# Memory projections in two rounded parts, the gate's products between two weight slots, and the band attention ahead of the sparse one

## The reference, cut to what matters

```python
k = (mem @ w_k).reshape(B, M, X_HEADS, X_HEAD_DIM)   # cross_attention, for both layers: 1024 -> 512
v = (mem @ w_v).reshape(B, M, X_HEADS, X_HEAD_DIM)
...
gate = jnp.einsum('gpq,bnqgc->bnpgc', sgu_w, vg) + sgu_b.T[None, None, :, :, None]   # ab_mixer
b_out = neighbourhood_attention(q_l, k_l, v_l, k_c, v_c, rel_bias)                   # reads v_l, v_c
...
def even_mixer(x, w_in, ckv_gain, w_uk, w_uv, sinks, w_out, rel_table):
    q_a, c_kv, q_i, k_i, w_i, q_b, k_b, v_b = split_cols(x @ w_in, EVEN_WIDTHS)
    o_a = dsa_attention(q_a, c_kv, q_i, k_i, w_i, ckv_gain, w_uk, w_uv, rel_table[:, :A_HEADS])
    o_b = banded_attention(q_b, k_b, v_b, rel_table[:, A_HEADS:A_HEADS + B_HEADS], B_WINDOW, sinks)
    return jnp.concatenate([o_a, o_b], axis=-1) @ w_out
```

## Time and profile before

| | |
|---|---|
| Median of three runs | 2578.78 us (2578.42 to 2579.43) |
| The profiled execution | 2579.02 us |
| Its span, first to last instruction | 2577.2 us |
| Mean granted TensorE clock | 0.993 of 2.4 GHz |
| PE busy | 2508.4 us, 97% of the span |
| DVE busy | 1984.1 us, 77% |
| ACT busy | 1164.9 us, 45% |
| Time outside the span | 2579.02 - 2577.2 = 1.8 us |

### The profile page before, as it was taken

How to read it: one execution, slowest core, us unless ns; L and a number is a source line. 1 busy time by engine, 2 the same in 40 slices (tenths; PEclk the granted TensorE clock), 3 DMA queues, 4 the chain that set the end, 5 groups by cost and what they waited for, 6 DMA issues and landing times.

```text
span 2577.2 us, 42769 instructions
## 1 busy us (share of the span) xinstructions
PE 2508.4 (97%) x16883; PEld 2143.3 (83%) x16883; DVE 1984.1 (77%) x2452; ACT 1164.9 (45%) x1477; POOL 87.5 (3%) x109
## 2 busy tenths in 40 slices
PE   9999999999999999889999899999999999999998
PEld 6786788888789999789998688888888888888886
DVE  0875877777776886858887747888889888988887
ACT  1427200000431003532013736777777777777776
POOL 0100100000000001000001100000000000000000
PEclk9999999999999999999999999999999999999999
DMA  8771454444315553224545124999899989999996
GB/s 346 275 268 61 156 180 166 166 170 163 115 50 220 185 186 135 80 101 156 185 179 197 34 99 167 374 366 376 331 376 362 374 335 372 366 351 357 363 374 252
DMA packets 90969, 603.85 MB, mean 234 GB/s; under 512 B 9792, under 2 KB 12864, under 8 KB 23616
## 3 DMA queue, kind: packets, MB, share of 16 engines
q1 hardware_dynamic: 77424, 544.24, 56.0%
q0 software_dynamic: 13392, 57.41, 6.2%
HBM read 598.47 MB, written 3.15 MB: 233 GB/s over the span
## 4 chain that ended last, share of the span: by engine, by line
PE 90%; DVE 5%; ACT 2%; issue 1%; DMA 1%; DVEq 0%; SPq 0%; ACTq 0%
PE bank L1143 12%; PE bank L1147 12%; PE bank L1146 12%; PE bank L2354 8%; PE bank L2358 8%; PE bank L2357 8%; PE bank L2385 4%; PE bank L2389 4%; PE bank L2388 4%; PE bank L516 2%; ACT arena L1423 1%; PE bank L1796 1%; PE bank L1399 1%; PE bank L1378 1%; PE bank L556 1%
## 5 line engine op out<-in xcount | busy, mean ns | idle before, releaser
L941 DVE TENSOR_TENSOR ring_part<-ring,arena_part 128x2048 fp32r<-128x2048 f32 (+1 forms) x478 | 1073.2, 2276 | 23.8 <-ACT arena_part L960 9.3
L2689 ACT ACTIVATE arena_part<-ring 128x2048 fp32r<-128x2048 f32 x339 | 647.2, 1920 | 196.8 <-DMA ring<-in_stream 196.6
L1143 PE MATMUL bank<-arena_part 128*128 128x256 f32 (+1 forms) x2024 | 644.9, 319 | 4.6 <-DVE ring_part L941 4.6
L1147 PE MATMUL bank<-arena_part,ring_part 128*128 128x256 f32 (+1 forms) x2024 | 643.2, 318 | 0.0
L1146 PE MATMUL bank<-h_part,arena_part 128*128 128x256 f32 (+1 forms) x1496 | 474.9, 317 | 0.0
L1143 PEld LDWEIGHTS bank<-arena_part 128*128 128x128 f32 x2024 | 385.9, 191 | 33.0 <-issue 6.8
L1147 PEld LDWEIGHTS bank<-arena_part,ring_part 128*128 128x128 f32 x2024 | 385.9, 191 | 25.4
L2354 PE MATMUL bank<-arena_part,h_part 128*128 128x512 f32 x896 | 354.5, 396 | 0.0
L2358 PE MATMUL bank<-arena_part,h_part 128*128 128x512 f32 x896 | 350.0, 391 | 0.0
L2357 PE MATMUL bank<-ring_part,h_part 128*128 128x512 f32 x896 | 349.2, 390 | 0.0
L1245 ACT ACTIVATE arena<-bank 128x256 f32<-128x256 f32 (+1 forms) x66 | 30.1, 455 | 636.8 <-PE bank L1147 635.9
(11 more groups left out here) (364 smaller groups left out, 3090.5 us busy)
## 6 DMA issues: line engine op xcount, KB each, us to landing
ring<-in_stream SPq DMA_DIRECT2D x515, 1024.0 KB, 4.9
arena<-in_ada_stream POOLq DMA_DIRECT2D x80, 512.0 KB, 4.5
consts<-in_small POOLq DMA_DIRECT2D x1, 2800.0 KB, 11.7
mem_store<-arena POOLq DMA_DIRECT2D x2, 1024.0 KB, 13.1
arena<-in_c_rows POOLq DMA_DIRECT2D x2, 1024.0 KB, 7.1
arena<-in_ab_bias POOLq DMA_DIRECT2D x1, 2048.0 KB, 10.1
arena<-in_t_bias POOLq DMA_DIRECT2D x1, 2048.0 KB, 8.7
arena<-in_mem_t SPq DMA_DIRECT2D x1, 1024.0 KB, 5.0
```

Source lines behind the costliest of these rows:

```text
L941: return nc.vector.tensor_tensor(low, value, high.bitcast(F32), ALU.subtract)
L1143: m = nc.tensor.matmul(out_ap, w_high, high, start=start, stop=False)
L1147: return nc.tensor.matmul(out_ap, w_low, high, start=False, stop=stop)
L2689: nc.scalar.activation(high, ring[:, where], ACT.Copy).then_inc(sem("moe_high"), 1)
```

## The change

What it does, piece by piece:

1. **Start.** The memory (`mem_in`) is parted into `mem_high` (ACT, eight pieces) and `mem_low` (DVE, eight pieces). Seven of the eight memory slots are parted too; K1a alone stays in f32. V1a and V1b are now loaded behind K1b and ahead of A0, and all four of these slots ahead of x and the context. The turned modulation rows stand between the two halves of the last value products.
2. **AB mixer.** The sixteen gate products stand between slots AB8 and AB9 of the value products, and DVE works on the gate ahead of copying the values out. The gate waits for its own weights (`sgu_landed`); the attention's first value step waits for the copied values.
3. **Even mixer.** `w_idx` is multiplied among the split products of the third and fourth column. The index scores follow at once on the column of c, ahead of its sum of squares. k_b and v_b are copied by ACT, not by DVE. The band's three steps stand first in the attention (`N_BAND`), and the latent values behind its last step, in two parts.

```diff
-START = ["K1a", "K1b", "A0", "A1", "V1a", "V1b", "A2", "A3", "A4", "K0a", "A5", "A6", "A7", "K0b", "V0a", "V0b"]
+START = ["K1a", "K1b", "V1a", "V1b", "A0", "A1", "A2", "K0a", "A3", "A4", "K0b", "A5", "A6", "A7", "V0a", "V0b"]
...
+                        if rounded:
+                            m = split_product(bk, w, PS[b][:, X2], mem_high[:, k, :], mem_low[:, k, :], k == 0, k == DC - 1,
+                                              highs=mem_slot_high)
+                            continue
...
-            mem_key_products(range(4))
+            mem_key_products(range(2), rounded=False)
+            pe.wait_ge(sem("mem_split"), DC)
+            mem_key_products(range(2, 4))
+            mem_value_products()
...
+            act.wait_ge(sem("mem_landed"), 16)
+            for c in range(DC):
+                nc.scalar.activation(mem_high[:, c, :], mem_in[:, c, :], ACT.Copy).then_inc(sem("mem_rounded"), 1)
+            for name in ("K1b", "V1a", "V1b"):
+                slot_high_act(bk, START.index(name), mem_slot_high, fresh=True)
             act.wait_ge(sem("x_landed"), 32)
             squares_act(bk, TT, lambda c: None)
+            slot_high_act(bk, START.index("K0a"), mem_slot_high, fresh=True)
             root_act(bk, TT, 0)
+            slot_high_act(bk, START.index("K0b"), mem_slot_high, fresh=True)
+            act.wait_ge(sem("mem_stored1"), 16)
+            for name in ("V0a", "V0b"):
+                slot_high_act(bk, START.index(name), mem_slot_high, fresh=True)
...
+            split_token_products(bk, w, ab_high, h_part, 4, ab_slot_high, between=gate_products)
+            for taken in queries_keys_taken:
                 pe.wait_ge(*taken)
...
+            attention_pe(bk, ab_steps(), values_ready)
...
-            attention_pe(bk, dsa_steps() + band_steps(), latent_values)
+            outs = attention_pe(bk, band_steps() + dsa_steps(), sparse_ready)
+            for j, taken in enumerate(outs):
+                pe.wait_ge(*bk.freed(taken))
+                b = bk.fill(score_bank(j))
+                pe.wait_ge(free(b), bk.emptied())
+                for h in range(4 * j, 4 * j + 4):
+                    at = SEQ * (h // 2 % 2)
+                    m = nc.tensor.matmul(PS[b][half(h % 2), at:at + SEQ], uv[:, h, :], o_lat[:, h, :], start=True, stop=True)
+                m.then_inc(full(b), 1)
...
+            for n in range(4):
+                load(n)
```

More of the change, by code:

```diff
@@ L297, in build @@
         mem_store = [nc.dram_tensor(f"mem_store{l}", (P, 2048), F32, kind="Internal").ap() for l in range(2)]
+        mem_high, mem_low = (part_area(at, 2048, "p (c t) -> p c t", c=DC) for at in (22368, 4096))
+        mem_slot_high = {START.index(name): part_area(at, SLOT) for name, at in (
+            ("K1b", 10240), ("V1a", 12288), ("V1b", 15360), ("K0a", 17408), ("K0b", 10240), ("V0a", 20320), ("V0b", 2048))}
         MEM_BANKS, MEM_GROUPS = (6, 7), 6
@@ L1179, in split_token_products @@
             for k in range(DC):
+                if between and k == DC // 2:
+                    between()
                 r, j = w.t // TILES, k % per
@@ L1788, in mem_key_products, with mem_value_products @@
                     m.then_inc(full(b), 1)
-            def mem_value_products():
-                parts = w.slots(2)
+            def mem_value_products(between=None):
+                begin = w.t // TILES
                 for t in range(2):
@@ L2910, in _ @@
             slot_low_dve(bk, AB_AT + 9, ab_slot_high)
-            slot_low_dve(bk, AB_AT + 10, out_slot_high)
-            for t in range(4):
-                to(v_att[:, t, :])
-            dve.wait_ge(sem("ab_landed"), 48)
+            dve.wait_ge(sem("sgu_landed"), 32)
+            values = [bk.next_bank() for _ in range(4)]
+            values_full = [bk.freed(bk.turn - 4 + t)[1] for t in range(4)]
             for g in range(4):
```

282 lines of the change are left out of this document (155 added, 127 removed).

## The result

The changed kernel takes 2566.16 us (median of 5, 2564.88 to 2567.68) against 2579.43 of the kernel before beside it: a ratio of 0.9948, 95% interval 0.9938 to 0.9959, 13.3 us less. The forecast was 2557, its range 2552 to 2566. The direction is right, and the median lies 0.2 over the range (two of the five executions, 2564.88 and 2565.31, lie in it); of the 21.7 us forecast 13.3 came, and that distance is what has to be explained.

The account below looks back on a forecast made before the run. PE, busy 2508.4 of 2577.2 us, was taken as the bound, with other limits at three places. Gains 11.6 + 3.7 + 6.9 = 22.2, less 0.5 for the clock: 2579.02 - 21.7 = 2557.3, say 2557; range 2552 to 2566.

Parts of the forecast that it names:

- The gate did not stop PE: Between AB8 and AB9: 2.3 us in hand, so no wait; the rival that PE waits there said 2585, chance 0.03.
- The failed step: Start, loads: at 420 to 430 GB/s, 2.5 us a slot, V0a lands at about 54.8 us.
- PE waits 1.8 there: Start, ahead of the V0 values: PE waits 1.8 us for V0a's low part, ready at 59.0.
- the sum gave back 0.5: Whole sum: 0.5 us deducted for a clock drop behind one of the start's new short waits.
- Loads behind 55 us: Start: a sign that the prediction is wrong, the start's loads landing later than 55 us.
- the start pays less: Start: V0a lands 2 to 3 us later, only 5 to 7 of 11.6 us come, 2562 to 2564; chance 0.15.
- The AB attention: Start of the AB attention: DVE's gate work leaves the path to the first softmax pass, gain 3.7 us.
- The even mixer: Even mixer up to its output products: gain 6.9 us, or 8.6 by the end of DVE's chain alone.
- Its work until the scaling of the last step is the same in another order, 24.7: Even attention: DVE's work from the first softmax pass to the last scaling stays 24.7 us, ending at 1082.0.
- I take 2.7, 0.9 gained: Even mixer: w_idx products cost 2.7 us among the others against 3.63 as a block, 0.9 gained.
- the 1.7 set there: Even mixer: a clock drop behind PE's wait, reaching over the first output products, costs up to 1.7 us.
- A long low clock in this attention: Even attention: a sign of being wrong, clock 0.5 for more than one spell; rival of lasting low clock, about 2570, chance 0.05.

Follow-up runs that it names:

- the store out of the way, late: Changed kernel with the 1 MB store of finished keys and values issued when PE has begun on V0b, not at 39.2 us: 2563.9 us, ratio 0.9941.
- between with nine fillers: Changed kernel with that store issued when PE begins on A7, plus 9 products on constants in PE's wait ahead of V0a: 2561.6 us, ratio 0.9925.
- its repeat: The changed kernel run again with nothing altered, with a second profiled execution: 2567.4 us, ratio 0.9954.
- the start alone: Kernel before with only part 1 of the change (memory products in rounded parts, new slot order, earlier loads): 2576.2 us, ratio 0.9981.
- the gate alone: Kernel before with only part 2 of the change (gate between AB8 and AB9, DVE's gate work ahead of the values): 2578.1 us, ratio 0.9985.
- the even part alone: Kernel before with only part 3 of the change (earlier columns and index scores, ACT copies, band steps first): 2572.5 us, ratio 0.9966.

## Why the prediction was wrong, and where it was right

**Right.** The work of PE at the start: values of the second cross attention ended at 34.4 (forecast 34.5), PE was ready for V0 at 57.3 (57.2). From DVE's addition to AB1 it was 17.7 (17.5). The gate did not stop PE. The mask ended 3.0 earlier within the even mixer (3.4). No table load came in. One sum is slightly off in itself: the pieces listed up to 57.2 add up to 56.95.

**The failed step** is the sentence "In full flow the queues bring 420 to 430 GB/s, 2.5 us a slot; with the seven slots and the store ahead of it V0a lands at about 54.8". V0a landed near 57.3. In place of full flow the trace shows queues that twice ran almost dry ahead of K0b, and the runs a store that took 3.0 and not the 2.5 of a load. The DMA's slices of 32 to 58 us (0.65 us each):

```profile
GB/s 25 189 38 429 403 466 139 151 328 403 429 391 416 403 378 315 315 227 403 416 416 391 441 454 416 441 403 403 391 441 416 492 403 416 429 403 429 416 416 441
```

In the first slices and again near 37 us they fall to 25 to 190 GB/s. A slot's load is issued when PE begins five slots on; PE was on the values of V1, each half of which needs both slots, until 34.4, and the loads of A3, A4 and K0b went out one by one, at 31.97, 35.49 and 36.34. From K0a's landing at 33.8 seven slots and the store, each at 2.5, would have given 53.8, and the forecast said 54.8; K0b, the third of the seven, was already 2.9 late at 44.2, and the store took 3.0 and not 2.5: 57.3. The store's part is shown by moving it, and the same run shows that K0b's delay isn't the store's. That this delay comes of the late issues is read from the trace; no run moved them. On top, "PE waits 1.8 there" became 4.45, and behind that wait the clock fell: 1.5 us, where the sum gave back 0.5. Loads behind 55 us were among the prediction's own signs of being wrong. Last, the values take 0.24 for each instruction and not 0.227: 0.3 in the first half (5.8 for 24 where the clock held). So rows were turned at 70.3, not 65.75, and all behind them, which has no slack as the prediction said, came 4.7 late. With the store out of the way, late or between with nine fillers, V0a landed at 54.3, the clock held, and AB0 and AB1 began at 71.42 and 83.6, where the forecast had 71.2 and 83.4. The rival "the start pays less", at 0.15, was the case, in its place and at its size; it was priced at 2562 to 2564 because it was taken alone.

**The AB attention**: right in its mechanism; DVE's four copies end 0.8 behind the first score (0.7), but its first pass comes 1.3 behind, since it then waits 0.52 for the scores themselves (191.16 above), a wait that the sum has not. 3.2 in place of 3.7, in two kernels.

**The even mixer**: the sum was near (5.3 in the profiled execution, 7.2 in its repeat, forecast 6.9), but by errors that cancel. "Its work until the scaling of the last step is the same in another order, 24.7" is wrong: the chain takes 26.5 with one spell of low clock, and 28.5 with a long one. PE's timeline shows why: the second transposes (1058.11) wait for ACT, which has the exponentials of a band step of eight pieces to do before its copy, and the next scores, queued behind them, keep DVE idle for 2.04 (1061.86). The order of the work on DVE was not what bound the filling of the pipeline. It also began 0.6 later than forecast, and one term ahead of it was wrong: of the w_idx products "I take 2.7, 0.9 gained", but from the third column to the fifth PE took 9.15 (994.53 to 1003.68), where two columns alone take 5.76. So the w_idx products cost 3.4 among the others, hardly less than the 3.63 of the block. Against that, the tail behind the last scaling was 6.5 and not 7.5, PE's wait ahead of the output products 1.34 and not 3, and they found the clock high: the 1.7 set there were paid 20 to 30 us earlier. A long low clock in this attention was among the signs of being wrong too. That these errors nearly cancel is luck.

**Outside the span**: 1.3 us that no term held. I had noted 1.8 us and taken it as fixed.

By size: 4.7 for the start, 0.5 for the AB attention, 1.6 for the even mixer, 0.4 between, 1.3 outside, less the 0.5 given back for the clock: 8.0, the distance from 21.7 to 13.7.

## What to carry to other kernels

A load's landing is worked out from when it can be issued, not from the full rate of the queues: list for each slot when its turn comes, and look for slices in which the queues run dry. When work ahead of a chain without slack is made shorter, price that chain's begin first, since each microsecond there counts in full; a transfer that nobody waits for can be moved out of the way, and a filler in a long wait that remains spares the products behind it the low clock (1.3 to 2.8 us here, behind waits of 4.45 to 5.32). A moved block with the same work is not the same chain: ask which engine fills the pipeline in the new order.

## What the hardware showed that I had not expected

- A fetch of instructions can be under way when the program is over. In the changed kernel 0.02 MB were fetched 1.9 us behind the last instruction, on q8, and the time was 2.4 to 3.1 us over the span in ten executions; with 40 more instructions at the end of PE's program there was no fetch, and it was 1.8 to 1.9. All changed kernels with 40 to 76 instructions more on PE were there, wherever these stood, the one with 18 more at 2.0, and those with none more, the start alone among them, at 2.5 to 3.2 (medians); the gate alone, the even part alone and the kernel before had 1.8. With 40 or more instructions added it was gone in all four, with 18 it came 1.2 us behind the end in place of 1.9; why one program has the fetch and another not is not shown.
- The clock falls for 3.4 us in stretches in which PE is busy throughout, in some executions and not in others (0.50 against 1.00 at 661.9 us). Ahead of V0a it fell behind all six waits of 4.45 to 5.32 us and behind one of 1.87, and held behind one of 1.39. The Trainium skill ("TensorE: Matmul & The Clock Gate", Part 1) says that the time at the lower clock when a kernel starts varies from run to run; these runs show such a variation in the middle of the program.
- A filler does not remove a spell by itself: with fillers in the waits of the even attention the clock fell at 1061.6, on products; the changed kernel's two executions without them had their spells from 1051.9 and from 1057.8.
